# ScalarE order around the last query block of a head pair, and products without a reader in TensorE's waits

## The reference, cut to what matters

```python
def _causal_attention(q, k, v):            # q, k: 96 a head, v: 64 a head
    for s, e in bounds:
        sc = einsum('bqhd,bkhd->bhqk', q[:, s:e], k[:, :e]) * scale
        sc = where(causal, sc, -inf)
        probs = softmax(sc, axis=-1)
        outs.append(einsum('bhqk,bkhd->bqhd', probs, v[:, :e]))

def layer(h):                              # twice
    p = h @ w_in                           # columns of RWKV, of attention, of two gates
    mixed = sigmoid(g1) * (rwkv(p) @ w1) + sigmoid(g2) * (attention(p) @ w2)
    h = layer_norm(ALPHA * h + mixed @ w_out)
    f = (silu(conv3(gate)) * conv3(val)) @ w_down      # gate, val = h @ w_up
    return layer_norm(ALPHA * h + f)
```

## Time and profile before

| what | value |
|---|---|
| median of the runs | 4064.2 us (4061.74 to 4066.52) |
| the profiled execution's own time | 4074.72 us |
| span of that execution, first to last instruction | 4072.9 us |
| TensorE matmuls busy | 3811.2 us (94%) |
| VectorE / ScalarE / GpSimd busy | 51% / 26% / 23% |
| granted TensorE clock, mean | 0.971 of full speed |

### The profile page before, as it was taken

How to read it: one execution, slowest core, us unless ns; L and a number is a source line. 1 busy time by engine, 2 the same in 40 slices (tenths; PEclk the granted TensorE clock), 3 DMA queues, 4 the chain that set the end, 5 groups by cost and what they waited for, 6 DMA issues and landing times. The chain is left out here.

```text
span 4072.9 us, 67363 instructions
## 1 busy us (share of the span) xinstructions
PE 3811.2 (94%) x28247; PEld 3479.4 (85%) x28247; DVE 2058.4 (51%) x2437; ACT 1067.1 (26%) x1505; POOL 948.9 (23%) x466
## 2 busy tenths in 40 slices
PE   6988999999998999999988889999999899999998
PEld 5565998887998999999975569898879899999997
DVE  2254447565555544444523444585655554544446
ACT  4255124223104112121132431341220231211123
POOL 4000320000442333333300004100014233333331
PEclk9988999999999999999998899999999999999999
DMA  4410246432411111111124102463323111111111
GB/s 108 121 51 25 78 134 190 129 77 77 133 45 32 47 47 42 47 47 42 51 49 121 54 27 94 136 197 99 87 93 111 31 42 48 47 42 47 46 44 52
DMA packets 362487, 304.66 MB, mean 75 GB/s; under 512 B 101403, under 2 KB 314615, under 8 KB 362215
## 3 DMA queue, kind: packets, MB, share of 16 engines
q1 hardware_dynamic: 341960, 248.82, 21.7%
q10 hardware_dynamic: 20255, 51.78, 3.4%
HBM read 218.55 MB, written 82.00 MB: 74 GB/s over the span
## 5 line engine op out<-in xcount | busy, mean ns | idle before, releaser
L243 POOL TENSOR_TENSOR w_hi<-w_raw,consts 128x1024 fp32r<-128x1024 f32 (+1 forms) x204 | 365.6, 1792 | 2660.3 <-PE psum L199 1644.7
L199 PE MATMUL psum<-h_hi,w_hi 128*128 128x348 f32 x3600 | 779.0, 325 | 29.8 <-ACT lat_sq L720 10.8
L199 PE MATMUL psum<-h_lo,w_hi 128*128 128x348 f32 x3600 | 770.4, 322 | 0.0
L199 PE MATMUL psum<-h_hi,w_lo 128*128 128x348 f32 x3600 | 769.0, 322 | 0.0
L199 PEld LDWEIGHTS psum<-h_hi,w_hi 128*128 128x128 f32 x3600 | 610.7, 190 | 37.9 <-ACT lat_sq L720 12.5
L199 PEld LDWEIGHTS psum<-h_lo,w_hi 128*128 128x128 f32 x3600 | 612.7, 189 | 0.0
L199 PEld LDWEIGHTS psum<-h_hi,w_lo 128*128 128x128 f32 x3600 | 607.8, 189 | 0.0
L245 POOL TENSOR_TENSOR w_lo<-w_raw,w_hi 128x1024 fp32r<-128x1024 f32 (+1 forms) x204 | 493.3, 2418 | 16.0
L2575 DVE SCALAR_TENSOR_TENSOR cv_g<-up_g,cw,cv_g 128x1044 f32<-128x1044 f32 x44 | 141.7, 3220 | 303.2 <-ACT cv_g L2447 303.2
L2557 DVE TENSOR_TENSOR acc<-acc,psum 128x1044 f32<-128x1044 f32 x176 | 217.8, 1237 | 142.5 <-PE psum L199 142.0
L199 PE MATMUL psum<-f_hi,w_hi 128*128 128x348 f32 x1056 | 227.8, 324 | 21.0 <-DVE acc L2557 21.0
(11 more groups left out here) (304 smaller groups left out, 5646.0 us busy)
## 6 DMA issues: line engine op xcount, KB each, us to landing
w_raw<-in_w_up SPq DMA_DIRECT2D x88, 512.0 KB
w_raw<-in_w_in SPq DMA_DIRECT2D x68, 512.0 KB
w_raw<-in_w_down SPq DMA_DIRECT2D x44, 512.0 KB
gate_scratch<-gst ACTq DMA_DIRECT2D x32, 522.0 KB, 3.0
gbuf<-gate_scratch SPq DMA_DIRECT2D x32, 522.0 KB, 3.6
prep_scratch<-prep ACTq DMA_DIRECT2D x8, 2080.0 KB
pc<-prep_scratch SPq DMA_DIRECT2D x20, 832.0 KB, 4.5
rkv_scratch<-mixed_p ACTq DMA_DIRECT2D x24, 522.0 KB, 4.2
```

Source lines behind the costliest of these rows:

```text
L199: last = nc.tensor.matmul(bank[:, n, :], w(k), x(k)[:, nrange(n)], start=(k == 0 and q == 0), stop=(k == kt - 1 and q == 2))
L243: nc.gpsimd.tensor_tensor(w_hi[s][:, 0:width], w_raw[s][:, 0:width], consts[:, 4:5].broadcast_to([P, width]), ALU.mult).then_inc(hi_done.s ...
```

## The change

Two things are done.

ScalarE's order over a boundary becomes: spread of a, exponent (b, 0), copies of T(b, 0), exponent (b, 1), copies of T(b, 1). So the spread goes ahead of the exponent of head 0, and the exponent of head 1 goes behind the copies of T(b, 0). In the other steps the order is as it was.

`keep_warm` is called in TensorE's list: 2 products before the third latent tile and 2 after the first sum of squares; 4 at the end of the latent phase; 3 after the first two scores of the attention; 2 at each boundary between B(a) and S(b, 1); 3 at the end of the RWKV columns; 2 after the last gate; 2 at the second stage of the scan; in each layer norm 2 after the mean and 8 after the last variance term (6 in the last norm of the kernel); 3 after the first two tiles of the up-projection; 4 between the two halves of the merge. That is 53 in layer 0 and 51 in layer 1. Two of the calls stand behind a wait that is added with them.

```diff
--- before.py
+++ after.py
@@ -676,10 +676,12 @@
                 def squares(t, n):
                     product32(pset[t % 2], [(ones[:, :], sq[i][:, :]) for i in range(2)]).then_inc(pe_tile, 1)
                 pe.sem_inc(used, 2)
+                keep_warm(7, 2)
                 pe.wait_ge(acts.sem, acts.of(0, "sq0"))
                 tile(2, 2)
                 pe.wait_ge(acts.sem, acts.of(0, "sq1"))
                 squares(3, 0)
+                keep_warm(7, 2)
                 pe.wait_ge(acts.sem, acts.of(0, "sq2"))
                 tile(3, 4)
                 pe.wait_ge(acts.sem, acts.of(0, "ln_q"))
@@ -710,6 +712,8 @@
                     for k in range(LT):
                         last = nc.tensor.matmul(psum[0:CH, 6 + c % 2, :], latent[:, LT + k, c * CH:(c + 1) * CH], w_uv[:, k, :], start=(k == 0), stop=(k == LT - 1))
                     last.then_inc(up_tile, 1)
+                pe.wait_ge(u_acts.sem, u_acts.of(0, f"cp{copied[-1]}"))
+                keep_warm(0, 4)
 
             @block.scalar
             def _(act):
@@ -830,23 +834,22 @@
         def by_act(e, q):
             return e == 1 or q != 1
 
-        def sp_first(t):
-
-            return late(t + 1) or t + 1 == NS
-
         pe_n, act_n, dve_n = ["S0_0", "S0_1"], ["exp0_0", "exp0_1"], []
         for e in range(2):
             dve_n += [f"mask0_{e}", f"max0_{e}"]
         for t, (g, i) in enumerate(steps):
             for e in range(2):
                 pe_n += [f"T{t}_{e}_{q}" for q, _ in groups(i)] + ([f"S{t + 1}_{e}"] if t + 1 < NS and not (e and late(t + 1)) else [])
-                act_n += [f"tc{t}_{e}_{q}" for q, _ in groups(i) if by_act(e, q)]
+                act_n += [f"tc{t}_{e}_{q}" for q, _ in groups(i) if by_act(e, q)] + ([f"exp{t}_1"] if e == 0 and late(t) else [])
                 dve_n += [f"tc{t}_{e}_{q}" for q, _ in groups(i) if not by_act(e, q)]
                 dve_n += [f"y{t - 1}"] if t and e == 0 and not late(t) else []
                 dve_n += [f"inv{t}", f"rb{t}"] if e == 0 else []
                 dve_n += [f"y{t}"] if e and late(t + 1) else []
                 dve_n += [f"mask{t + 1}_{e}", f"max{t + 1}_{e}"] if t + 1 < NS else []
-            act_n += ([f"exp{t + 1}_0"] if t + 1 < NS else []) + ([f"sp{t}"] if sp_first(t) else []) + ([f"exp{t + 1}_1"] if t + 1 < NS else []) + ([] if sp_first(t) else [f"sp{t}"])
+            if late(t + 1):
+                act_n += [f"sp{t}", f"exp{t + 1}_0"]
+            else:
+                act_n += [f"exp{t + 1}_{e}" for e in range(2)] + [f"sp{t}"] if t + 1 < NS else [f"sp{t}"]
             pe_n += [f"O{t}", f"B{t}"] + ([f"S{t + 1}_1"] if late(t + 1) else [])
         dve_n.append(f"y{NS - 1}")
         with Phase(nc, "pe_steps", "act_steps", "dve_steps", "qk00_in", "qk01_in", "qk10_in", "qk11_in", "v00_in", "v01_in", "v10_in", "v11_in", "y0_stored", "pads",
@@ -959,6 +962,7 @@
 
                 scores(0, 0)
                 scores(0, 1)
+                keep_warm(7, 3)
                 for t in range(NS):
                     for e in range(2):
                         flips(t, e)
@@ -1003,14 +1008,16 @@
                         for q, blocks in groups(i):
                             if by_act(e, q):
                                 flip_copy(act, lambda o, x: nc.scalar.activation(o, x, ACT.Copy), acts, t, e, q, blocks)
+                        if e == 0 and late(t):
+                            exponent(t, 1)
+                    if late(t + 1):
+                        spread_out(t)
+                        exponent(t + 1, 0)
+                        continue
                     if t + 1 < NS:
                         exponent(t + 1, 0)
-                    if sp_first(t):
-                        spread_out(t)
-                    if t + 1 < NS:
                         exponent(t + 1, 1)
-                    if not sp_first(t):
-                        spread_out(t)
+                    spread_out(t)
 
             @block.vector
             def _(dve):
@@ -1398,6 +1406,8 @@
                     else:
                         free = (acts.sem, acts.of(0, f"g{u - 2}"))
                     gate(u, pset[u % 2], free)
+                pe.wait_ge(acts.sem, acts.of(0, f"pa{RT - 1}_21"))
+                keep_warm(7, 2)
 
             @block.scalar
             def _(act):
@@ -2045,11 +2056,13 @@
             for c in range(NB):
                 last = nc.tensor.matmul(n.mean_bank[:, c, :], ones[:, :], acc[:, KD - 1, nrange(c)], start=False, stop=True)
             n.pe.did(last, "mean")
+            keep_warm(6, 2)
             for k in range(KD):
                 pe.wait_ge(n.act.sem, n.act.of(0, f"sq{k}"))
                 for c in range(NB):
                     last = nc.tensor.matmul(n.var_bank[:, c, :], ones[:, :], lsq[k % 2][:, nrange(c)], start=(k == 0), stop=(k == KD - 1))
                 n.pe.did(last, f"v{k}")
+            keep_warm(7, 6 if n.final else 8)
 
         def norm_act(act, n):
             for k in range(KD):
@@ -2254,6 +2267,7 @@
                     if isinstance(i, int):
                         pe.wait_ge(split.sem, split.of(u + 2))
                         two_products(w_hi, w_lo, tile_ready, lambda last, s: pes.did(last, f"{'gv'[s]}{B}0"))
+                        keep_warm(6, 3)
                     for s in range(2 if isinstance(i, int) else 0, UP):
                         pair, x_ = s // 2, "gv"[s % 2]
                         pe.wait_ge(split.sem, split.of(u + (s + 1)))
@@ -2346,6 +2360,7 @@
                 with pe.Fori(0, HALF - 1) as i:
                     for s in range(2):
                         merged(i * 2 + (2 + s), s, RT, y_hi, y_lo, (m0s.sem, m0s.of(i, f"z{s}")))
+                keep_warm(6, 4)
                 for s in range(2):
                     merged(KD + s, s, RT, x_hi, x_lo, (m0s.sem, m0s.of(HALF - 1, f"z{s}")), x_ready if s == 0 else None)
                 with pe.Fori(0, HALF - 1) as i:
```

## The result

Four runs of the changed kernel took 4016.26 to 4025.26 us, median 4021.94, beside 4065.36 (4061.74 to 4067.64) for the kernel before: a ratio of 0.9892 with a 95% interval of 0.9876 to 0.9908. It is faster by 1.1%, five times what the measurement can tell. The forecast was 4008 and the range 3988 to 4042. The profiled execution took 4025.26 us, span 4023.5, so the profiles differ by 49.4 us of span where the sum said 56.

The account below looks back on a forecast made before the run. TensorE's low clock, plus the waits that left it idle before, was taken as the attention's bound. Terms 25.8 (six boundaries) + 8 (first boundaries) + 22 (outside) = 56 us, from 4064.2 to 4008; range 3988 to 4042.

Parts of the forecast that it names:

- rival of no effect: Whole kernel: gains from ScalarE's order and losses from late products cancel, 4060 us; chance 0.05.
- the slower one: At the waits: products run late at 1.2 GHz, 29 us lost less 11 from ScalarE's order, 4082 us; chance 0.07.
- R2: Low stretches hide behind other engines; only ScalarE's order counts, 15 us plus 5 outside, 4044 us; chance 0.10.
- A second fall costs the 2.25 us above ... I take it for two boundaries in three: Wait for exponent (b, 1) at six later boundaries: clock falls again, mean cost 1.5 us, leaving 25.8 us gained.
- R1: Clock falls again behind every boundary and first boundaries open low; 34 us gained, 4030 us; chance 0.18.
- a boundary's 6.25 us: B(a) to B(b) at high clock: gains 0.66, 1.90, 1.44 and 2.25 us, of 16.69 us.
- Outside the attention ... 22 us: Low stretches outside attention, both layers: 28 us if falls do not happen, four fifths taken, 22 us.
- The opening of the gates' phase: Gates' opening: gives 1.8 us, less 1 us since three products end just when the barrier would open, 0.8.
- The first norm: First layer norm: half of TensorE's busy time in its low stretch comes back, 2.3 us a layer.
- First boundaries: First boundary of each layer, from the attention's opening: 4 us each, 8 together, at best 6.8 each.
- the weak case of that step: Layer's first scores: clock low again in 2 us left idle, three products cost 4.7 us, little gain left.
- the good one: Layer's first boundary at high clock: three products end 2.4 us after S, gain at best 6.8 us.

Follow-up runs that it names:

- moved kernel: Against the changed kernel, the merge's four products moved from between its halves to the wait ahead of the output projection's tiles; 4007.5 us, ratio 0.9859.
- trimmed kernel: Changed kernel without the merge's four products, the three ahead of the r, k, v phase, and the two behind the gates' opening with their wait; 4029.8 us.

## Why the prediction was right or wrong

**What held.** The forecast's mechanism was the clock, and the low clock's length fell by two thirds. At the boundary the steps came as worked out: S(b, 1) 2.00 us for 2.03, T(b, 1)'s start 1.27 us behind the exponent's for 1.28, 10.32 us over all for 10.4. The price of one product was 0.74 us for 0.80. The rival of no effect and the slower one are out. R2, that the clock is not the price, is out as well: the order alone would then have given 15 us and gave 33 by its ratio. The first boundaries show the price by themselves (below).

**"A second fall costs the 2.25 us above ... I take it for two boundaries in three"**: this step failed. No second fall came at any steady boundary of the changed kernel. The idle time itself was sized nearly right, 1.5 us of 3.0: it was 1.39 us, in two pieces of 0.25 (the row at 246.48) and 1.14 (at 248.32). What failed is what I read from rows 6, that such a wait brings the clock down at two boundaries in three: with this attention it did so at 3 of 48 in eight profiled kernels. Attention as a whole: 42.9 us where 33.8 were forecast, the steady ones 35.6 for 25.8. R1 was the same fear and is out here; it came true at all six with the products alone and at four of the six with the order alone. The Trainium skill's rule of the short idles (TensorE: Matmul & The Clock Gate, "A second HAM failure mode: psum-queue depth-cycling") agrees with the products-only run, where a wait of 2.53 us stood before the fall, and not with the changed kernel, where 1.14 us between groups was borne at 1.00. The same 1.14 us stood before the three falls named above, so by these runs the length of the wait alone does not decide.

**The attribution inside the boundary.** I gave 2.10 of a boundary's 6.25 us to the order (0.66 for the earlier scores and 1.44 behind the exponent) and the other 4.15 to the clock held by the two products. The runs show that the order takes 1.5 us out of each of the two waits, and with it alone the clock stayed up through S(b, 1) at all six steady boundaries and through the whole of two of them; the products add 2 to 3 us over six boundaries (2.1 against the order alone, 2.9 against none at a boundary).

**"Outside the attention ... 22 us"**: 6.5 measured. Three parts of it failed. The merge was put at +2.7 us a layer from a wait that its products do not fill, and they stand on the path with 2.8 us each time. Moved into the wait, the stretch gave 3.9 us in layer 0 and 2.1 in layer 1, near the term; in the three other kernels with them moved it gave 0.2 to 4.0, so the agreement is partly luck.

The opening of the gates' phase was given 0.8. The three products ahead of it cost 0.9 us a layer, as the sum had it (1 us), but of the 1.8 us set against that only 0.1 and 0.5 came back. The rest of the r, k, v phase's loss in layer 0 is the fall at its opening. The loss in the gates' phase comes some 60 us ahead of the two products there, in a wait for ScalarE that was 0.61 us before and is 1.86 in the changed kernel, with the clock falling behind it:

```profile
722.06 0.98 PE L1380 MATMUL psum<-prep 64*104 64x104 f32 x16 [1.86 <-ACT adg L1437]
...
723.80 1.07 PE L199 MATMUL psum<-h_lo,w_hi 128*128 128x348 f32 x3
```

Kernels with equal code came out from -6.4 to +3.1 us there (both layers, with the scan's opening), so why the wait grows stays open.

The first norm was to give 2.3 us a layer and gave 0.6 and 0.5, and the norm that ends layer 0 gave 0.4 for 2.1; of the 7.58 us of idle time 1.99 were left, and the clock fell once more in front of the up-projection:

```profile
1207.15 5.75 PE L220 MATMUL psum<-pair_mask,ident 104*104 104x416 f32 x16
...
1214.89 1.21 PE L213 MATMUL psum<-h_hi,w_hi 128*128 128x348 f32 x3 [1.99 <-DVE h_lo L2099]
```

The tiles of 1.21 us are as long as in the earlier trace rows: the products moved the fall, they did not remove it. In layer 0 the latent tiles (1.3 and 1.4 us for 1.4 and 1.7), the second pair of up-tiles (1.5 for 1.7), the variance products of the last norm (1.7 for 1.7) and the scan (0.8 in its opening and 1.6 in its second stage for 1.5) were right or better.

**First boundaries.** 8 us forecast, 7.3 measured, but unevenly: 5.7 in layer 0 and 1.6 in layer 1. So the term came near by a mean of two unlike cases, which is luck. TensorE's rows at the opening of both layers:

```profile
187.09 3.95 PE L220 MATMUL psum<-pair_mask,ident 104*104 104x416 f32 x6
190.88 0.26 PE L938 MATMUL psum<-ident,pr 116*116 116x116 f32 x1
...
2163.68 1.10 PE L924 MATMUL psum<-kh,qh 96*116 96x116 f32 x4 [2.06 <-SPq L881]
2164.57 4.37 PE L220 MATMUL psum<-pair_mask,ident 104*104 104x416 f32 x6
```

The three products took 3.95 and 4.37 us, at the low clock for all or most of them (1.46 us each, for a bound of 1.56). This was the weak case of that step, and it came in both layers; in layer 0 the clock rose right behind the three and 5.7 us were gained all the same. The moved kernel's layer 1 had the good one, 2.26 us for the three and 7.3 us gained. Over the sixteen first boundaries of the eight kernels with this attention the gain goes with the low clock's length in it: 7.3 us where it never fell, 5.4 to 5.7 with 3.4 us of low clock, 3.7 to 4.2 with 6.8 us, and 1.6 to 2.9 with 10.2 us.

## What to carry to other kernels

Look at every wait between the engine's high clock and the next burst, not at the first one: a faster start runs into the next wait earlier and makes it longer, and here a changed order that shortened both was worth three quarters of the gain, with no work added. A filler product is free only inside a measured wait, and it is a cost where the clock would have stayed up without it; give each its own row, with the wait's releaser, before placing it, and count falls over several profiles before keeping it. When a small edit moves a stage whose code is the same, compare the instruction fetches of that stage before explaining it.

## What the runs showed that I had not expected

A loop's time depends on where it stands in TensorE's program. The feed-forward loops took 748.0 to 749.0 us with 9 or 10 instruction fetches (0.15 or 0.16 MB), 750.7 and 752.3 us with 18 and 28, 753 to 757 us with 45, and 773.4 us with 46 in the trimmed kernel, where a stop of 2.4 to 2.7 us came once a pass and took the clock with it; 24 instructions of shift moved it by 25 us. The Trainium skill (Advanced Engine Details and Errata, "ISA Cache") gives TensorE 128 KB for instructions, in lines of 16 KB or 256 instructions. The loop's body has 1772 (TensorE's records in one pass of the trace), 6.9 lines, so it comes near the whole and may touch one line more or less by its place; that this decides is not shown. The size of a fetch in the traces (46 of them 0.75 MB) agrees, and so do the seven fetches of the first pass. The same section also says "Only 2 cache lines!"; the four passes without a fetch speak against that for TensorE. Which places are short was only read off the runs, and one of them (the kernel with one product at a boundary) did not keep to it.

The same code at the first boundary of a layer gained anything from 1.6 to 7.3 us. In a kernel that is at the edge of the clock's fall, a single profile is no basis for a term of 2 or 3 us.
